# An MoE layer's experts: from split weights in three passes to unsplit fp32 weights on column tiles of 32

## The chip, the cores and the metric

The kernel runs on one NeuronCore of a Trainium2 chip. The time is that of the device, in microseconds, from launch to end: 1814.1 us, the median of three runs (1814.04, 1814.10 and 1815.13). The other seven cores do nothing. The engines are named as in the profile: PE is TensorE (matmul), PEld its loading of stationary operands, DVE is VectorE, ACT is ScalarE, POOL is GpSimd, SP is SyncE, which issues most DMAs.

## The reference

One layer: a mixer (gated linear attention and dilated attention), a router that picks 4 of 32 experts for each of 512 tokens, the experts, and a norm, all in fp32. The change touches only the experts:

```
h = xb @ w_gate_up[e] + b_gate_up[e]          # 1024 -> 2048
gate = min(h[:, ::2], 7);  up = clip(h[:, 1::2], -7, 7)
act = (up + 1) * (gate * sigmoid(1.702 * gate))
y = act @ w_down[e] + b_down[e]               # 1024 -> 1024
```

Each token's four results are weighted by its gates and added to its residual row. An expert has 12 MB of weights, 32 experts have 384 MB, and each is used by the 64 tokens that chose it on average (at most 96 in the first pass; more would go through a second path that this input does not take).

## The kernel before

The program has a mixer stage (to about 612 us), a routing part, and from 672 us the expert stage.

**Exact fp32 out of a faster type.** The mixer and the experts hold operands as float32r, which is rounded, so each fp32 operand is split in two: `hi` (the rounded value) and `lo` (the rest). A product is three passes: x_hi by w_hi, x_lo by w_hi, x_hi by w_lo. For weights the splitting costs one ACT copy (`hi`, line 1731) and one DVE subtraction (`lo`, line 1736) for every chunk of 128 x 2048 elements (1 MB).

**Chunks.** The weights of an expert come in 12 chunks: 8 of gate-up (128 input rows by 2048 outputs) and 4 of down (2 x 128 input rows by 1024 outputs). SP loads them in order into a ring of 8 buffers, `expert_chunk` (`RING`), and ACT and DVE split each into one of 4 pairs of buffers (`SLOTS`). SP may load chunk c once `lo` of chunk c-8 is done.

**Products.** `gate_up_chunk` (lines 1888, 1891) does 12 matmuls: three passes over four banks of 512 columns, with the transposed rows of the expert (`rowsT_hi`, `rowsT_lo`, 128 x 128) stationary. `down_chunk` (lines 1901, 1906) does 12 too. `turn_rows` (1852) and `turn_act` (1860) transpose the gathered rows and the activations on PE, 8 blocks of 96 each; ACT and DVE take the results out of PSUM as hi and lo. `gate_up_bias` (1881) starts the four banks with the bias.

**Bodies.** The order of work of each engine is written out by hand in `body_pe`, `body_act`, `body_dve` and the `body` functions of SP and POOL. Body e computes gate-up of expert e+1 (q = 0 to 7) and down of expert e (q = 8 to 11), and the gating of e in between. Body 0 and body 1 are written out, bodies 2 to 29 are seven turns of a loop of four bodies (`over_bodies`), body 30 is written out, and the down product of expert 31 is the last.

**Lists and rows.** The routing writes each choice (token, weight) by an indirect DMA into a table in DRAM; 16 such DMAs (`list_place`, line 1766) run on POOL at the start of the expert stage, and then the lists of all experts are read back (line 2114). From then on `list_take` on DVE gives an expert's row numbers, `gather` on POOL (1782) fetches its rows, and `scatter` (1845) adds its 96 result rows of 1024 to the residual in DRAM, one indirect DMA for each expert.

**Around it.** `mix_and_route` holds the end of the mixer, the router and the first loads of weights; `no_work` products fill PE where it would wait.

## Time and profile before

| | |
|---|---|
| median of three runs | 1814.1 us |
| profiled execution | span 1814.6 us from first to last instruction (its own time is not given apart) |
| PE busy, PEld busy | 98%, 81% of the span |
| DVE, ACT, POOL busy | 76%, 61%, 8% |
| granted PE clock | 0.993 of full speed over the span |
| moved by DMA | 497.5 MB, 274 GB/s over the span, 379 GB/s from 900 to 1700 us |
| L1736 DVE, the `lo` of the chunks | 384 of 2286 ns, 864.8 us |
| L1731 ACT, the `hi` of the chunks | 384 of 1916 ns, 735.2 us |

A busy PE is a chain of matmuls whose durations overlap: one of 512 columns is shown with some 390 ns, while the next starts 227 ns after it. So the pace of PE is read from the start times of the timeline and not from the mean of one. The name `128*128 128x512` says: a stationary operand of 128 rows by 128 columns, a moving operand of 128 by 512.

### The profile page before, as it was taken

To read this page: it belongs to the slowest core of one execution; us is meant where nothing else is said; L and a number is where in the kernel's file an instruction comes from. 1 tells how busy PE (TensorE), PEld (TensorE's weight loads), DVE (VectorE), ACT (ScalarE), POOL (GpSimd) and SP (SyncE) were. 2 spreads that over 40 slices of the span, in tenths; PEclk is the share of its full clock that TensorE was granted. 3 is DMA by queue.
4 is the path that set the end of the run, shared out by engine and by line. 5 is a ranking of instruction groups with operands and counts; after the bars stand their busy time and mean duration, and the time that the engine had idled before them with its cause. 6 is when DMAs were issued, how large, how long until landed. Compare 5 with 4: busy or idle time off the path is not lost.

```text
span 1814.6 us, 24657 instructions
## 1 busy us (share of the span) xinstructions
PE 1781.8 (98%) x9023; PEld 1469.6 (81%) x9024; DVE 1386.3 (76%) x1169; ACT 1100.3 (61%) x994; POOL 139.8 (8%) x120
## 2 busy tenths in 40 slices
PE   9999999999999999999999999999999999999996
PEld 7877788898888877788888888888888888888885
DVE  4256255537324568999999999999999999999997
ACT  4253222247422346677777777777777777777774
POOL 1000000000000026100000000000000000000001
PEclk9999999999999999999999999999999999999998
DMA  5321354312223659999999999999999999999993
GB/s 187 125 93 47 112 142 123 110 53 85 86 99 133 226 214 318 370 370 378 386 374 370 385 378 375 379 385 369 381 384 376 375 387 375 380 384 372 383 379 123
DMA packets 101688, 497.53 MB, mean 274 GB/s; under 512 B 15819, under 2 KB 17867, under 8 KB 52033
## 3 DMA queue, kind: packets, MB, share of 16 engines
q1 hardware_dynamic: 90960, 478.01, 69.2%
q0 software_dynamic: 9616, 16.62, 3.6%
q10 hardware_dynamic: 1056, 2.16, 0.5%
q8 instruction: 36, 0.59, 0.1%
q14 instruction: 20, 0.16, 0.0%
HBM read 484.85 MB, written 25.21 MB: 281 GB/s over the span
## 4 chain that ended last, share of the span: by engine, by line
PE 59%; POOL 1%; DVE 1%; DMA 1%; issue 1%; ACT 0%; DVEq 0%; POOLq 0%
PE psum L1888 24%; PE psum L1901 13%; PE psum L1891 12%; PE psum L1906 6%; POOL slots_of_experts L1766 1%; PE psum L1860 1%; PE psum L1852 1%; PE psum L1881 1%; DVE expert_lo L1736 0%; DMA slots_of_experts<-choice_token_and_weight,choice_row_of_table 0%; DMA lists_of_experts<-slots_of_experts 0%; DVE expert_chunk L2042 0%; DVE h_sb L2210 0%; POOL total_rstd L2129 0%; PE psum L2031 0%
## 5 line engine op out<-in xcount | busy, mean ns | idle before, releaser
L1736 DVE TENSOR_TENSOR expert_lo<-expert_chunk,expert_hi 128x2048 fp32r<-128x2048 f32 x384 | 864.8, 2286 | 45.7 <-ACT expert_hi L1731 43.8
L1731 ACT CAST expert_hi<-expert_chunk 128x2048 fp32r<-128x2048 f32 x384 | 735.2, 1916 | 227.3 <-PE psum L1891 170.6
L277 DVE TENSOR_TENSOR chunk_lo<-chunk,chunk_hi 128x2048 fp32r<-128x2048 f32 x48 | 110.0, 2292 | 259.0 <-ACT chunk_hi L273 240.2
L1888 PE MATMUL psum<-expert_hi,rowsT_hi 128*128 128x512 f32 x992 | 268.6, 393 | 0.0
L1891 PE MATMUL psum<-expert_lo,rowsT_hi 128*128 128x512 f32 x992 | 265.8, 390 | 0.6 <-DVE expert_lo L1736 0.6
L1888 PE MATMUL psum<-expert_hi,rowsT_lo 128*128 128x512 f32 x992 | 265.6, 390 | 0.0
L1891 PEld LDWEIGHTS psum<-expert_lo,rowsT_hi 128*128 128x128 f32 x992 | 186.1, 188 | 40.0 <-DVE expert_lo L1736 1.7
L1888 PEld LDWEIGHTS psum<-expert_hi,rowsT_lo 128*128 128x128 f32 x992 | 186.4, 188 | 39.2
L1888 PEld LDWEIGHTS psum<-expert_hi,rowsT_hi 128*128 128x128 f32 x992 | 184.0, 188 | 36.6 <-issue 0.2
L273 ACT CAST chunk_hi<-chunk 128x2048 fp32r<-128x2048 f32 x48 | 91.8, 1913 | 189.8 <-PE psum L308 158.0
L1901 PE MATMUL psum<-expert_hi,activationsT_hi 128*128 128x512 f32 x496 | 157.6, 399 | 0.0
L308 PE MATMUL psum<-xT_hi,chunk_hi 128*128 128x512 f32 x384 | 151.2, 394 | 4.6 <-DVE chunk_lo L277 2.1
L1901 PE MATMUL psum<-expert_hi,activationsT_lo 128*128 128x512 f32 x496 | 154.0, 392 | 0.0
L308 PE MATMUL psum<-xT_lo,chunk_hi 128*128 128x512 f32 x384 | 150.4, 392 | 0.0
L308 PE MATMUL psum<-xT_hi,chunk_lo 128*128 128x512 f32 x384 | 150.1, 391 | 0.0
L1906 PE MATMUL psum<-expert_lo,activationsT_hi 128*128 128x512 f32 x496 | 132.9, 390 | 0.1
L308 PE MATMUL psum<-chunk_hi,xT_hi 128*128 128x512 f32 x288 | 113.7, 395 | 2.6 <-ACT gla_v L710 1.5
L308 PE MATMUL psum<-chunk_hi,xT_lo 128*128 128x512 f32 x288 | 112.8, 392 | 0.0
L308 PE MATMUL psum<-chunk_lo,xT_hi 128*128 128x512 f32 x288 | 112.7, 391 | 0.0
L1901 PEld LDWEIGHTS psum<-expert_hi,activationsT_hi 128*128 128x128 f32 x496 | 91.2, 189 | 24.8 <-issue 6.9
L1901 PEld LDWEIGHTS psum<-expert_hi,activationsT_lo 128*128 128x128 f32 x496 | 93.8, 189 | 20.0
L1906 PEld LDWEIGHTS psum<-expert_lo,activationsT_hi 128*128 128x128 f32 x496 | 93.1, 188 | 19.9 <-DVE expert_lo L1736 0.5
(295 smaller groups left out, 1938.6 us busy)
## 6 DMA issues: line engine op xcount, KB each, us to landing
expert_chunk<-in_expert_w_gate_up SPq DMA_DIRECT2D x256, 1024.0 KB, 7.7
expert_chunk<-in_expert_w_down SPq DMA_DIRECT2D x128, 1024.0 KB, 6.9
chunk<-in_w_in SPq DMA_DIRECT2D x38, 1024.0 KB, 5.0
chunk<-in_w_branch_gla SPq DMA_DIRECT2D x4, 1024.0 KB, 5.0
chunk<-in_w_mix_out SPq DMA_DIRECT2D x4, 1024.0 KB, 5.0
gla_v<-in_x SPq DMA_DIRECT2D x4, 512.0 KB, 9.8
y_glaT_away<-h_sb SPq DMA_DIRECT2D x1, 2048.0 KB, 10.9
att_qT_then_y_glaT<-y_glaT_away SPq DMA_DIRECT2D x1, 2048.0 KB, 8.3
```

Source lines behind the costliest of these rows:

```text
L273: act.copy(self.whi[c][:], self.raw[c][:]).then_inc(self.hi_done[c], 1)
L277: dve.tensor_tensor(self.wlo[c][:], self.raw[c][:], self.whi[c][:].bitcast(F32), ALU.subtract).then_inc(self.lo_done[c], 1)
L308: last = pe.matmul(bank, stationary, moving, start=(k == 0 and n == 0), stop=(k == KT - 1 and n == 2))
L1731: act.copy(self.expert_hi[c % self.SLOTS][:], self.expert_ring[c % self.RING][:]).then_inc(self.moe["hi"], 1)
L1736: dve.tensor_tensor(self.expert_lo[s][:], self.expert_ring[c % self.RING][:], self.expert_hi[s][:].bitcast(F32), ALU.subtract).then_inc(se ...
L1766: pool.indirect_dma_start(self.table, bass.IndirectOffsetOnAxis(ap=self.address[:, b, j:j + 1], axis=0), self.record[:, b, j, :], None, bo ...
L1852: last = pe.transpose(turned(f)[:, k, :], rows[taken, (HALF_KT * f + k) * P:(HALF_KT * f + k + 1) * P], self.ident[taken, taken])
L1860: last = pe.transpose(turned(f)[:, k, :], a[taken, (HALF_KT * f + k) * P:(HALF_KT * f + k + 1) * P], self.ident[taken, taken])
L1888: pe.matmul(bank, x[:, k, :], whi[s][:, m // 2, m % 2 * COLS:(m % 2 + 1) * COLS], start=False, stop=False)
L1891: last = pe.matmul(bank, rows_hi[:, k, :], wlo[s][:, m // 2, m % 2 * COLS:(m % 2 + 1) * COLS], start=False, stop=(k == KT - 1))
L1901: pe.matmul(bank, x[:, 2 * q + kk, :], whi[s][:, kk, m * COLS:(m + 1) * COLS], start=(q == 0 and kk == 0 and x is acts[0]), stop=False)
L1906: last = pe.matmul(bank, acts[0][:, 2 * q + kk, :], wlo[s][:, kk, m * COLS:(m + 1) * COLS], start=False, stop=(q == 3 and kk == 1))
```

## The change

The weights of the experts are no longer split. PE multiplies them as fp32, and the stationary operand is a group of 32 token rows instead of 128: `FIRST_SLOTS` is 96, so there are three groups (`GROUPS`), and for each group four products stand side by side on four column tiles of the array (`PARTS`), each with its own block of the weights as moving operand and its own 32 partitions of one PSUM bank as output. Gate-up moves 512 columns for each, down 256.

- `hi`, `lo`, their buffers and the hi/lo copies of rows and activations are gone; ACT alone takes transposed rows and activations out of PSUM. The ring has 16 buffers instead of 8, and SP waits for PE's use of chunk c-16 (`used`) instead of `lo` of c-8.
- The outputs now lie by part of the columns: partition 32p+r, group j holds token 32j+r and part p. So the gating works on 128 x 768 instead of 128 x 1024 elements, `turn_act` is six blocks of 128 (four behind q = 2, two behind q = 3), and the result rows leave in pieces of 256 columns: three indirect DMAs for each expert, which add to a residual seen as 2048 rows of 256. The row numbers of the pieces come from four more reads of the lists and one DVE operation.
- The last expert's down product stays row by row (96 stationary columns, 512 moving, fp32), for its result is added through one-hot products.
- In `mix_and_route`, SP loads three chunks when the first half of the last mixing product is done, three more behind the last bank, and two at the start of the expert stage, and no chunk is split there.

```diff
-                for c in range(1, self.SLOTS):
-                    self.hi(act, c)
...
-    RING, SLOTS = 8, 4
+    RING = 16
...
+    PARTS, GROUPS = P // QUARTER, FIRST_SLOTS // QUARTER
+    PIECE = D_MODEL // PARTS
...
+    def chunk_here(self, pe, c, i=0):
+        pe.wait_ge(self.chunk_loaded[c % self.RING], 16 * (self.PER_TURN // self.RING) * i + 16 * (c // self.RING + 1))
+        return self.expert_ring[c % self.RING]
...
+        def scatter(pool, e, u):
+            pool.wait_ge(S["y_out"], G * e + G)
+            pool.wait_ge(S["pieces"], 2 * e + 2)
+            pool.wait_ge(S["scattered"], 16 * G * e)
+            for j in range(G):
+                pool.sem_inc(S["passed"], 1)
+                pool.indirect_dma_start(pieces, bass.IndirectOffsetOnAxis(ap=self.piece_row[u][:, j:j + 1], axis=0),
+                                        y[:, j * PIECE:(j + 1) * PIECE], None, bounds_check=self.last_piece, oob_is_err=False,
+                                        compute_op=ALU.add).then_inc(S["scattered"], 16)
...
+        def gate_up_chunk(pe, c, i, k, x=xT):
+            w = chunk_here(pe, c, i)
+            for j, bank in enumerate(h_banks):
+                for p in range(PARTS):
+                    last = pe.matmul(bank[part_rows(p), :], x[:, k, part_rows(j)], w[:, p // 2, p % 2 * COLS:(p % 2 + 1) * COLS],
+                                     start=False, stop=(k == KT - 1))
+            last.then_inc(S["used"], 1)
+
+        def down_chunk(pe, c, i, q):
+            w = chunk_here(pe, c, i)
             for kk in range(2):
...
+                for j in range(G):
+                    for p in range(PARTS):
+                        last = pe.matmul(y_of(j)[part_rows(p), :], aT[:, q, kk, part_rows(j)], w[:, kk, p * PIECE:(p + 1) * PIECE],
+                                         start=(q == 0 and kk == 0), stop=(q == 3 and kk == 1))
+            last.then_inc(S["used"], 1)
...
+        def last_down_chunk(pe, c, q):
+            w = chunk_here(pe, c)
             for kk in range(2):
...
+                for m, bank in enumerate(last_banks):
+                    last = pe.matmul(bank[taken, :], as_act(xT)[:, q, kk, :], w[:, kk, m * COLS:(m + 1) * COLS],
+                                     start=(q == 0 and kk == 0), stop=(q == 3 and kk == 1))
+            last.then_inc(S["used"], 1)
...
-                        sp.wait_ge(S["lo"], TURN * i + c - RING + 1)
+                        sp.wait_ge(S["used"], TURN * i + c - RING + 1)
...
+                for p in range(PARTS):
+                    pool.dma_start(self.piece_lists[part_rows(p)].rearrange("p j e n -> p j (e n)"),
+                                   self.table[E:(FIRST_SLOTS + 1) * E, :].rearrange("(j p e) n -> p j (e n)", j=G, e=E)
+                                   ).then_inc(S["lists_in"], 16)
```

On PE, in body 1 (gate-up of expert 2), stood before, from the second chunk to the fifth:

```order
L1888 MATMUL psum<-expert_hi1,rowsT_hi 128x512 x4
L1888 MATMUL psum<-expert_hi1,rowsT_lo 128x512 x4
L1891 MATMUL psum<-expert_lo1,rowsT_hi 128x512 x4
L1888 MATMUL psum<-expert_hi2,rowsT_hi 128x512 x4
L1888 MATMUL psum<-expert_hi2,rowsT_lo 128x512 x4
L1891 MATMUL psum<-expert_lo2,rowsT_hi 128x512 x4
L1860 MATMUL psum<-identity_sb,h_sb 128x96 x8
L1888 MATMUL psum<-expert_hi3,rowsT_hi 128x512 x4
L1888 MATMUL psum<-expert_hi3,rowsT_lo 128x512 x4
L1891 MATMUL psum<-expert_lo3,rowsT_hi 128x512 x4
```

and now, from the second chunk to the fifth (an output of 32 partitions, 12 products for each chunk; line 1888 is now `turn_act`):

```order
L1915 MATMUL psum<-expert_chunk5,rowsT 32x512 x12
L1915 MATMUL psum<-expert_chunk6,rowsT 32x512 x12
L1888 MATMUL psum<-identity_sb,h_sb 128x128 x4
L1915 MATMUL psum<-expert_chunk7,rowsT 32x512 x12
L1888 MATMUL psum<-identity_sb,h_sb 128x128 x2
L1915 MATMUL psum<-expert_chunk_late0,rowsT 32x512 x12
```

The 12 products of a chunk are as many as before; the transposes are split over two places. On PE, around the rows of the next expert and its bias in the same body (the down chunks), there stood before:

```order
L1906 MATMUL psum<-expert_lo1,activationsT_hi 128x512 x4
L1852 MATMUL psum<-identity_sb,h_sb 128x96 x8
L1881 MATMUL psum<-bias_rows1,ones_r 128x512 x4
L1901 MATMUL psum<-expert_hi2,activationsT_hi 128x512 x2
L1901 MATMUL psum<-expert_hi2,activationsT_lo 128x512 x2
```

and now:

```order
L1924 MATMUL psum<-expert_chunk_late3,activationsT 32x256 x24
L1924 MATMUL psum<-expert_chunk_late7,activationsT 32x256 x24
L1878 MATMUL psum<-identity_sb,h_sb 128x96 x8
L1908 MATMUL psum<-bias_rows1,bias_place_r 128x512 x3
L1924 MATMUL psum<-expert_chunk_late4,activationsT 32x256 x24
L1924 MATMUL psum<-expert_chunk_late5,activationsT 32x256 x24
```

A down chunk is 24 products of 256 columns, and the bias three products. On POOL, from the lists to the first scatter, there stood before:

```order
L2103 MEMSET activationsT_hi 128x8x32
L2103 MEMSET activationsT_lo 128x8x32
L2103 MEMSET rowsT_hi 128x8x32
L2103 MEMSET rowsT_lo 128x8x32
L1766 DMA slots_of_experts<-choice_token_and_weight,choice_row_of_table 4128x2 x4
L1782 DMA h_sb<-normed_rows,row_index 128x1024
L1766 DMA slots_of_experts<-choice_token_and_weight,choice_row_of_table 4128x2 x12
L2114 DMA lists_of_experts<-slots_of_experts 128x64
L1782 DMA h_sb<-normed_rows,row_index 128x1024 x2
L1845 DMA residual_rows<-h_sb,row_index 512x1024
```

and now:

```order
L1776 DMA slots_of_experts<-choice_token_and_weight,choice_row_of_table 4128x2 x4
L1796 DMA h_sb<-normed_rows,row_index 128x1024
L1776 DMA slots_of_experts<-choice_token_and_weight,choice_row_of_table 4128x2 x12
L2131 DMA lists_of_experts<-slots_of_experts 128x64
L2134 DMA lists_by_quadrant<-slots_of_experts 32x3x64 x4
L1796 DMA h_sb<-normed_rows,row_index 128x1024
L1870 DMA residual_rows<-h_sb,piece_row 2048x256 x3
```

The clearing of unused slots is gone, the lists are read five times, and the scatter of body 0 stands in body 0 and no longer in body 1.

## Rows read from the trace of the kernel before

**Rows 1.** the page: busy time and share of the span of each engine
```profile
PE 1781.8 (98%) x9023; PEld 1469.6 (81%) x9024; DVE 1386.3 (76%) x1169; ACT 1100.3 (61%) x994; POOL 139.8 (8%) x120
```

**Rows 2.** windows: stretch, length, busy us (instructions) per engine, PEclk, DMA share, GB/s
```profile
625.00:640.00 15.00, 15.00 (x71) 12.61 (x70) 10.01 (x17) 8.36 (x17) 2.09 (x2) 1.00 1.01 423
1200.00:1300.00 100.00, 100.00 (x476) 82.35 (x475) 95.58 (x65) 75.82 (x54) 7.88 (x6) 1.00 0.99 379
```

**Rows 3.** timeline, PE, one body: start us, us, engine, line, operation
```profile
1202.67 0.82 PE L1860 MATMUL psum<-identity_sb,h_sb 96*128 96x96 f32 x8
1206.11 1.07 PE L1888 MATMUL psum<-expert_hi,rowsT_hi 128*128 128x512 f32 x4
1208.83 1.07 PE L1888 MATMUL psum<-expert_hi,rowsT_hi 128*128 128x512 f32 x4
1222.43 0.82 PE L1852 MATMUL psum<-identity_sb,h_sb 96*128 96x96 f32 x8
1223.19 0.50 PE L1881 MATMUL psum<-bias_rows,ones_r 32*128 32x512 f32 x4
1237.36 0.82 PE L1860 MATMUL psum<-identity_sb,h_sb 96*128 96x96 f32 x8
```

**Rows 4.** timeline, PE, line 556: fp32 products on tiles of 64 columns
```profile
169.81 0.38 PE L556 MATMUL psum<-w_lr,gla_qkT 128*64 128x256 f32 x1
169.81 0.38 PE L556 MATMUL psum<-scan_keep_sb,gla_qkT 128*64 128x256 f32 x1
170.02 0.38 PE L556 MATMUL psum<-w_lr,gla_qkT 128*64 128x256 f32 x1
```

**Rows 5.** timeline, PE, lines 1048, 1015 and 1020: tiles of 64 and 32 columns
```profile
382.49 0.40 PE L308 MATMUL psum<-chunk_hi,xT_lo 128*128 128x512 f32 x1
382.82 0.71 PE L1015 MATMUL psum<-att_kT_window,att_qT_window 64*32 64x256 f32 x20
383.45 0.71 PE L1020 MATMUL psum<-att_kT,att_qT_then_y_glaT 64*128 64x128 f32 x8
...
400.99 1.09 PE L1048 MATMUL psum<-qk_halves_then_probsT,att_v 128*64 128x128 f32 x24
403.30 0.33 PE L1032 MATMUL psum<-identity_sb,att_negated 128*128 128x128 f32 x1
```

**Rows 6.** timeline, PE: router products and transposes on the whole array
```profile
642.08 1.87 PE L1414 MATMUL psum<-router_w_sb,chunk 128*128 128x32 f32 x16
643.78 1.19 PE L1403 MATMUL psum<-identity_sb,h_sb 128*128 128x128 f32 x8
644.72 0.47 PE L308 MATMUL psum<-chunk_hi,xT_hi 128*128 128x512 f32 x1
```

**Rows 7.** waits of SyncE, 860 to 1780: us in total, times, longest us
```profile
SPq L1726 <- DVE expert_lo L1736: 692.4, 314, 4.1
```

**Rows 8.** DMA queues, 900 to 1700: packets, MB, share of 16 engines
```profile
q1 hardware_dynamic: 40211, 290.51, 92.5%
q0 software_dynamic: 6727, 12.35, 6.0%
q14 instruction: 1, 0.01, 0.0%
```

**Rows 9.** timeline, PE, at the start of the expert stage
```profile
672.84 0.51 PE L1881 MATMUL psum<-bias_rows,ones_r 32*128 32x512 f32 x4 [0.93 <-PEq L139]
703.25 1.20 PE L1888 MATMUL psum<-expert_hi,rowsT_hi 128*128 128x512 f32 x4
```

**Rows 10.** timeline, POOL: two of the 16 DMAs of line 1766
```profile
682.23 0.98 POOL L1766 DMA_INDIRECT slots_of_experts<-choice_token_and_weight,choice_row_of_table  x1 [0.30 <-issue]
709.41 3.03 POOL L1766 DMA_INDIRECT slots_of_experts<-choice_token_and_weight,choice_row_of_table  x1 [0.30 <-issue]
```

**Rows 11.** timeline, PE and POOL: the last expert's down product and the last scatter
```profile
1783.69 0.62 PE L1901 MATMUL psum<-expert_hi,rowsT_hi 128*128 128x512 f32 x2
1785.96 2.18 POOL L1845 DMA_INDIRECT residual_rows<-h_sb,row_index  x1 [9.70 <-ACT h_sb L1950]
```

More of the change, by code:

```diff
@@ L93, in shape_constants @@
     c["bias_row"] = e
+    c["quadrant"] = (np.arange(P) // QUARTER).astype(np.float32)[:, None].copy()
+    place = np.zeros((P, P), np.float32)
+    for g in range(FIRST_SLOTS // QUARTER):
+        for part in range(P // QUARTER):
+            place[g * QUARTER + 2 * part:g * QUARTER + 2 * part + 2, part * QUARTER:(part + 1) * QUARTER] = 1.0
+    c["bias_place"] = place
     return c
@@ L1326, in _ @@
                 for b in range(NB):
+                    if b == NB - 1:
+                        sp.wait_ge(R["halfway"], 1)
+                        for q in range(3):
+                            self.load_gate_up(sp, self.body_chunk(0, q), 1, q)
                     sp.wait_ge(self.bank_free[b], last_mix + 1)
@@ L1330, in _ @@
                     sp.dma_start(self.normed[b * P:(b + 1) * P, :], hn[b]).then_inc(self.normed_stored, 16)
+                sp.wait_ge(self.bank_full[NB - 1], last_mix + 1)
+                for q in range(3, 6):
+                    self.load_gate_up(sp, self.body_chunk(0, q), 1, q)
             @block.gpsimd
@@ L1719, in load_bias_rows @@
         rows = self.bias_rows[u % 2]
-        for s in range(2):
-            sp.dma_start(rows[s:P:P // 4, :], self.bias_table[bass.ds(e, 1), :, s, :].rearrange("a m n -> (a m) n")
+        for j in range(self.GROUPS):
+            sp.dma_start(rows[j * QUARTER:j * QUARTER + 2 * self.PARTS, :],
+                         self.bias_table[bass.ds(e, 1), :, :, :].rearrange("a m s n -> (a m s) n")
                          ).then_inc(self.bias_in[u % 2], 16)
@@ L1854, in turn_rows, with turn_act @@
                 last.then_inc(S["x_turned"], 1)
-        def turn_act(pe, e):
+        def turn_act(pe, e, groups):
             pe.wait_ge(S["act"], e + 1)
-            for f in range(2):
-                for k in range(HALF_KT):
-                    last = pe.transpose(turned(f)[:, k, :], a[taken, (HALF_KT * f + k) * P:(HALF_KT * f + k + 1) * P],
-                                        self.ident[taken, taken])
-                last.then_inc(S["act_turned"], 1)
-        def turned_hi(act, e, in_bank, done, dst):
-            for f in range(2):
-                act.wait_ge(in_bank, 2 * e + f + 1)
-                act.copy(dst[:, HALF_KT * f:HALF_KT * (f + 1), taken], turned(f)).then_inc(done, 1)
@@ L1895, in down_chunk @@
-        def down_chunk(pe, c, i, q, banks=y_banks, acts=self.actT):
-            s = c % SLOTS
-            pe.wait_ge(S["hi"], TURN * i + c + 1)
-            for kk in range(2):
-                for x in acts:
-                    for m, bank in enumerate(banks):
-                        pe.matmul(bank, x[:, 2 * q + kk, :], whi[s][:, kk, m * COLS:(m + 1) * COLS],
-                                  start=(q == 0 and kk == 0 and x is acts[0]), stop=False)
-            pe.wait_ge(S["lo"], TURN * i + c + 1)
+            for j in groups:
+                if j >= 2:
+                    pe.wait_ge(S["aT_out"], G * e + j - 1)
+                for k in range(2):
+                    last = pe.transpose(turned_act(j)[:, k * P:(k + 1) * P], a[:, (2 * j + k) * P:(2 * j + k + 1) * P],
+                                        self.ident[:])
+                last.then_inc(S["act_turned"], 1)
@@ new lines, in down_chunk @@
+        def down_chunk(pe, c, i, q):
+            w = chunk_here(pe, c, i)
+            for kk in range(2):
+                for j in range(G):
+                    for p in range(PARTS):
[4 more added lines that the diff above has]
+            w = chunk_here(pe, c)
@@ L1904, in down_chunk @@
             for kk in range(2):
-                for m, bank in enumerate(banks):
-                    last = pe.matmul(bank, acts[0][:, 2 * q + kk, :], wlo[s][:, kk, m * COLS:(m + 1) * COLS], start=False,
-                                     stop=(q == 3 and kk == 1))
-            last.then_inc(S["slots_free"], 1)
+                for m, bank in enumerate(last_banks):
+                    last = pe.matmul(bank[taken, :], as_act(xT)[:, q, kk, :], w[:, kk, m * COLS:(m + 1) * COLS],
+                                     start=(q == 0 and kk == 0), stop=(q == 3 and kk == 1))
@@ L2030, in hi_products @@
                 pe.wait_ge(S["y_hi"], m + 1)
-                pe.matmul(sums[b][:, m, :], hotT[:, b, :], y_hi[:, m * COLS:(m + 1) * COLS], start=False, stop=False)
+                pe.matmul(sums[b][:, m, :], hotT[taken, b, :], y_hi[taken, m * COLS:(m + 1) * COLS], start=False, stop=False)
         def lo_products(pe, b):
@@ L2035, in lo_products @@
                 pe.wait_ge(S["y_lo"], m + 1)
-                last = pe.matmul(sums[b][:, m, :], hotT[:, b, :], y_lo[:, m * COLS:(m + 1) * COLS], start=False, stop=True)
+                last = pe.matmul(sums[b][:, m, :], hotT[taken, b, :], y_lo[taken, m * COLS:(m + 1) * COLS], start=False, stop=True)
             last.then_inc(S["totals"], 1)
```

333 lines of the change are left out of this document (150 added, 183 removed).

## The prediction

> **What bounds the kernel now.** I read the page first: PE is busy for 98% of the span [rows 1]. Then the windows, because the experts take 1,110 us of the span and a mean over all stages hides them. In 100 us of the expert loop PE is busy for 100.00, DVE for 95.58 and ACT for 75.82, and the granted clock is 1.00, the 2.4 GHz level [rows 2]. The DMA share of 0.99 looks like a second bound, so I read the waits: SP stood 692.4 us, 314 times, waiting for a free buffer [rows 7]. A loader that waits is not the bound; its transfers wait for their turn in the queues' time. In the mixer the same queues moved 423 GB/s, against 379 here [rows 2]. So PE sets the pace, DVE is close behind, and the DMA has some 10% in hand.
>
> The pace comes from start times, since the records of matmuls overlap. One body, from one transposing of activations to the next, is 1237.36 − 1202.67 = 34.69 us. A chunk of weights is 1208.83 − 1206.11 = 2.72 us. Twelve chunks are 32.64, and 2.05 are left for transposes and bias (1223.19 − 1222.43 = 0.76 for the rows alone) [rows 3].
>
> **What an fp32 product costs.** Two places in the mixer show it. On two tiles of 64 columns, two products of 256 columns start together at 169.81 and the next at 170.02 [rows 4]: about 0.213 us for one pass over 256 columns. Line 1015 issues 10 products in the code and shows 20 records [rows 5], so an fp32 product is two passes. These ten hold 2,048 columns (six of 256, four of 128); in two passes one after another they would take 4,096/256 × 0.213 = 3.4 us, but the next line starts 0.63 us after them (383.45 − 382.82). So tiles with different weights and different moving data do run side by side, 5.4 at once here.
>
> **The change part by part.**
>
> *Gate-up chunk.* Three groups × two passes × 512 columns, four tiles at once: 6 × 0.43 = 2.58 us. *Down chunk:* two halves × three groups × two passes × 0.215 = 2.58. Both were 2.72. The array does less work than 12 passes of split products by about 5%, if four tiles always stand side by side.
>
> *Rest of a body.* Six transposes of 128: eight of them took 644.72 − 643.78 = 0.94 us [rows 6], so six take 0.71. The rows' transposes stay at 0.76. The bias is three products that take a step of 0.43 if their twelve records pair up as in a chunk. New are three returns between the whole array and tiles of 32. At 382.49 a whole-array product was followed by tiles after 0.33 us [rows 5], against 0.227 for a product of its size (2.72/12), so 0.1 at least; I take 0.25 each for a drain and a first weight load that nothing covers, 0.75 in all. Body: 12 × 2.58 + 0.71 + 0.76 + 0.43 + 0.75 = 33.6 us. With 0.1 or 0.45 for a return it is 33.2 or 34.2.
>
> *DVE and ACT.* Per chunk a DVE subtraction of 2.3 us and an ACT copy of 1.9 go (384 of each). Neither sets the pace before, so it earns nothing by itself, but DVE has room for whatever the new gating needs. The gating handles 128 x 768 elements instead of 128 x 1024, in a body where DVE and ACT now idle for most of the time.
>
> *SP and the ring.* SP waits for PE's chunk c−16 instead of `lo` of c−8: 16 chunks of lead are over 40 us at 2.58 a chunk. The loads per body are 12 MB; at 423 GB/s they take 12 × 1.049/0.423 = 29.7 us, and at the packets' own share (92.5% of 800 us for 290.51 MB [rows 8]) 32.0. Gathers and scatters add 6.0% of 34.69 = 2.1 [rows 8]. So the queues need 31.8 to 34.1 us for a body and PE 33.6. That is the closest second, and the ring covers its jitter.
>
> *Start.* The bias products stand at 672.84 and wait for their sequencer, and body 0 begins at 703.25 [rows 9]. Expert 0's eight chunks end 8 × 0.14 = 1.1 us sooner, and the transposes and first chunk need no splitting by ACT and DVE ahead (about 1 us for the first): I take −2.5, with −1 and −4 as ends. The lists: one of POOL's 16 placing DMAs took 0.98 us, another 3.03 where DVE was subtracting [rows 10]. With most subtractions gone the list is out some 8 us sooner. Reading it five times instead of once adds four issues of about 1 us; the rows of the next expert are needed only in the middle of body 0, so this hides. If the 8 us don't come, about 3 us of body 0 stand open.
>
> *Bodies.* The last down product starts at 1783.69 [rows 11]: 1783.69 − 703.25 = 1,080.4 us for 31 bodies, or 31 × 34.69 + 5.0 of waits. Afterwards 31 × 33.6 = 1,041.6: −38.8 against the whole, if the 5 us of waits go with their cause; at 33.2 it is −51, at 34.2 −20.
>
> *Tail.* The last down product is now 16 products of 512 columns in fp32: 16 × 2 × 0.43 = 13.8 us against 4 × 2.72 = 10.9, +2.9, and +0.3 for changes of tile. The scatter before the last (one issue, 2.18 us, after 1783.69 [rows 11]) becomes three of 256 columns. Two more issues put its end some 4 to 5 us later in a tail of 1814.6 − 1783.69 = 30.9 us, in which PE's 13.8 come first; I count it hidden, with 1.5 us in hand, and +3 as its price if not.
>
> *Code.* Each half of a product is a weight load and a matmul of its own, and smaller tiles need four times as many: 12 chunks × 24 or 48 passes make some 384 pairs in a body against 144 + transposes. Before, the queue of instructions moved one packet in 800 us [rows 8], so code fetched at the loop's turns cost PE nothing visible. With twice the code a turn can need a fetch that PE waits for. The nearest row for such a wait is 0.93 us on PE's sequencer [rows 9]; I take 1.2 for each of six turns, +7, with 0 and 20 as ends. The Trainium skill (Runtime: NRT & Kernel Launch, Instruction fetch mechanics) says that PE's instruction memory holds 2,048 instructions and that a taken branch to a target outside the window must fetch before it goes on. By that rule the four bodies of a turn did not fit before either, yet no row here shows a stall, so it changes only the weight of a rival below.
>
> *Sum.* 1814.6 − 2.5 − 38.8 + 2.9 + 0.3 + 7 = 1783.5 in the profiled execution's terms (span 1814.6). The median of the runs is 0.5 lower: 1783 to 1784, say 1784. Bounds of the costs above give 1770 to 1795.
>
> **The rivals.**
>
> *A. Refetch at each turn.* Every turn of the loop waits for its first code and once or twice again: 3.3 us × 6 = 20 instead of 7. That gives 1797. For: the code grows. Against: one instruction packet in 800 us [rows 8].
>
> *B. Issue of pairs decides: slower.* A down chunk needs 48 pairs of weight load and matmul in 2.58 us, one per 54 ns; gate-up needs one per 107. The point from which it decides is 54 ns, and the gain is eaten at about 60: 192 down pairs × 6.4 ns = 1.2 us of each body. Against it: between 400.99 and 403.30 PE passed the 24 records of line 1048 and, as after 382.82, the 20 and 8 of lines 1015 and 1020: 52 pairs in 2.31 us, or 44 ns each [rows 5]. For it: the eight records of line 1020 fill about 0.65 us (81 ns each), what is left of the 2.31 when 24 and 20 take some 1.66 of it, and 16 router products of just 32 columns took 642.08 to 643.78, 1.70 us, 106 ns each, far more than their columns [rows 6]. At 81 ns a body is 192 × 0.027 = 5.2 us longer: +161, near 1945. Were it 62 ns, a body would grow by 192 × 0.008 = 1.6 and the whole come to 1833. The Trainium skill (TensorE: Matmul & The Clock Gate, Wait — 56ns, not 53.3ns?) gives about 62 ns per matmul for a sequencer without hardware decode and a floor near 25 with it; the 44 ns above speak for the second.
>
> *C. Tiles not side by side all the time.* If the weight load of a tile can't hide under that tile's own product (32 columns, some 55 ns), each of the 8 × 6 + 4 × 12 = 96 steps of a body pays: 5.3 us a body, near 1945. If only two tiles ran at once, a body would double, to over 2,700. Rows 5 speak against both.
>
> *D. The DMA becomes the bound.* 34.1 us at the upper end is 0.5 above PE: +16, about 1800. It is dear only if a scattered piece of 1 KB costs the queues as much as a row of 4 KB, for there are now four times as many: then scatters alone grow from about 1.3 to 5 us, a body is 38, and the time near 1860.
>
> *E. A wait once a body.* A chain of gather, scatter or gating that was covered comes late by about 1 us in each: 1784 + 31 = 1815, in the band 1805 to 1830. For: three scatters on POOL, each with a wait. Against: POOL is busy for 8% [rows 1], and DVE and ACT have more room than before.
>
> **How the numbers follow.** Forecast 0.56 (1770 to 1795), A 0.12, B 0.09, C 0.06, D 0.08, E 0.09. The likeliest gives 1784. The range: 1764 below, a body of 33.2 and no cost of code, less a few us for the start; 1836 above, which takes in A, E, the mild half of D and B at 62 ns, and leaves about 0.18 out above. A measurement of this kernel can tell 0.2%, that is 3.6 us. Faster: 0.56 + 0.12, a third of D and less than half of E, with some of B's lower end, 0.77 to 0.78. Same: 0.04, the part of E near 1814. Slower: the rest, 0.18.
>
> **What would show it.** Starts of the activation transposes 33.6 us apart; chunks 2.58 apart; in a chunk four products starting together, every 0.43 us in gate-up and 0.215 in down (not together: C; a down chunk longer than a gate-up chunk: B). SP's waits now on PE and long; if they vanish and PE waits for chunks, D. Instruction packets inside the loop with gaps in PE at the turns, 1 us each, or 3 in A. PE waiting for ACT, DVE or POOL once a body is E. The tail from the last down product's start 33 to 34 us instead of 30.9. Wrong altogether would be a body above 34.69.

## The result, and the profile after

The changed kernel takes 1831.2 us (median of four runs, 1829.6 to 1832.8) against 1814.6 for the kernel before (1814.0 to 1816.3). The ratio is 1.0092, with a 95% interval of 1.0078 to 1.0106: slower by 0.9%, where 1784 was forecast. The profiled executions have spans of 1831.0 and 1814.6 us, so 16.4 us are to be explained, and 47 between the forecast (1783.5 in these terms) and the result.

The page of the kernel after, first the busy line, then the queues:

```profile
span 1831.0 us, 38017 instructions
...
PE 1767.4 (97%) x16447; PEld 996.1 (54%) x16448; DVE 449.8 (25%) x692; ACT 378.9 (21%) x673; POOL 218.1 (12%) x182
...
q1 hardware_dynamic: 92272, 479.12, 68.4%
q0 software_dynamic: 18672, 16.74, 4.5%
...
q8 instruction: 140, 2.29, 0.5%
```

DVE and ACT are nearly free, as expected; PE is not [rows 1]. The last line is code: 140 packets of 16 KB, for which the prediction had budgeted 7 us. Between 900 and 1700 us the kernel before moved one instruction packet [rows 8]; this one moved 87:

```profile
q1 hardware_dynamic: 39985, 284.29, 90.2%
q0 software_dynamic: 12680, 11.73, 7.2%
q8 instruction: 86, 1.41, 0.7%
q14 instruction: 1, 0.01, 0.0%
```

An average body says little here, so I listed the distance between the first transposes of successive bodies. Before, it is 34.7 from body 1 on. After, it is 33.6, except at six places, one behind each turn of the loop but the last: 41.5, 40.5, 42.2, 39.7, 41.5 and 41.0 us. The timeline of PE, first an ordinary body (the products of the next would start at 1198.2 by the same pattern), then what stands at a turn of the loop:

```profile
1172.35 0.66 PE L1888 MATMUL psum<-identity_sb,h_sb 128*128 128x128 f32 x4
1172.94 2.78 PE L1915 MATMUL psum<-expert_chunk,rowsT 128*32 128x512 f32 x24
1175.65 0.44 PE L1888 MATMUL psum<-identity_sb,h_sb 128*128 128x128 f32 x2
1176.02 10.51 PE L1915 MATMUL psum<-expert_chunk_late,rowsT 128*32 128x512 f32 x96
1186.35 5.36 PE L1924 MATMUL psum<-expert_chunk_late,activationsT 128*32 128x256 f32 x96
1191.64 0.88 PE L1878 MATMUL psum<-identity_sb,h_sb 96*128 96x96 f32 x8
1192.45 0.50 PE L1908 MATMUL psum<-bias_rows,bias_place_r 32*128 32x512 f32 x3
1192.88 5.39 PE L1924 MATMUL psum<-expert_chunk_late,activationsT 128*32 128x256 f32 x96
1204.60 1.93 PE L1915 MATMUL psum<-expert_chunk,rowsT 128*32 128x512 f32 x8 [6.33 <-issue]
```

(The last row is cut by the window; the start time and the wait are what is read.) Four gate-up chunks take 1186.35 − 1176.02 = 10.33, 2.58 each, and two down chunks 5.29, 2.65 each. Then PE stands still for 6.33 us, and what ended the wait is "issue": no semaphore, no engine, no DMA of data.

What PE was doing is on record one level lower. Every engine closes a turn with a branch instruction (COMPARE_BRANCH, on the line of the loop). The trace gives, for the six jumps back, the shortest, median and longest duration in ns. First the kernel before, then the kernel after, PE and for comparison ACT:

```profile
L2051 PEldq COMPARE_BRANCH  x6: 211/211/224, 913.0 to 1606.9; - x6
```

```profile
L2065 PEldq COMPARE_BRANCH  x6: 5557/6034/7367, 913.4 to 1622.4; - x6
L2065 ACTq COMPARE_BRANCH  x6: 45/45/50, 915.1 to 1624.1; - x6
```

Of the engines only PE is held at the jump (DVE, POOL and SP take under 0.1 us for theirs too). Its branch takes 0.21 us before and 5.6 to 7.4 after, 6.16 on the mean. When the branch begins, 20 matmul records are still ahead of it and last another 1.36 us; the rest is the wait that the timeline shows, 4.5 to 6.3 us. In each of these branches one packet of code begins 3.2 to 5.0 us after the branch (917.21 for the one at 913.42), takes about 1 us, and the branch ends some 1.4 to 1.5 us after it (919.55).

At the turn near 915 the wait is 5.06 us. The windows there (columns as in rows 2):

```profile
914.00:920.00 6.00, 0.94 (x20) 0.37 (x16) 0.00 (x0) 1.20 (x3) 2.63 (x2) 0.88 1.00 388
920.00:925.00 5.00, 5.00 (x28) 1.21 (x28) 0.00 (x0) 0.00 (x0) 3.12 (x3) 0.50 0.50 83
925.00:930.00 5.00, 5.00 (x52) 1.38 (x44) 0.00 (x0) 0.00 (x0) 0.00 (x0) 0.97 0.75 253
```

PE had been idle for 5 us, and the granted clock then is 0.50, the 1.2 GHz level, for the five microseconds in which PE works again: 28 matmul records (two for each fp32 product) instead of some 46. So a turn costs the wait and then another 1.7 to 2.9 us, 2.4 on the mean.

The other loss is ahead of the loop. Timeline of PE in the gate-up of expert 0:

```profile
687.27 7.56 PE L1915 MATMUL psum<-expert_chunk,activationsT 128*32 128x512 f32 x63
695.22 1.08 PE L1915 MATMUL psum<-expert_chunk,activationsT 128*32 128x512 f32 x5 [0.38 <-issue]
696.66 1.06 PE L1915 MATMUL psum<-expert_chunk,activationsT 128*32 128x512 f32 x4 [0.37 <-issue]
698.08 0.49 PE L1878 MATMUL psum<-identity_sb,h_sb 96*128 96x96 f32 x4 [0.35 <-issue]
700.20 0.64 PE L1878 MATMUL psum<-identity_sb,h_sb 96*128 96x96 f32 x3 [1.63 <-issue]
701.63 0.32 PE L1878 MATMUL psum<-identity_sb,h_sb 96*128 96x96 f32 x1 [0.80 <-issue]
702.35 8.27 PE L1915 MATMUL psum<-expert_chunk,activationsT 128*32 128x512 f32 x48 [0.40 <-issue]
...
713.13 1.06 PE L1915 MATMUL psum<-expert_chunk_late,rowsT 128*32 128x512 f32 x8
```

From 694.8 to 702.3 PE's products come in handfuls with waits on nothing visible between them. SP stops as well: the chunk of SP's next load was free from 692.6 on, and the load was issued at 700.93. In these 7 us the queues move next to nothing, so it is no lack of bandwidth (the last columns are the granted clock, 0.86, the DMA share, 0.21, and 46 GB/s):

```profile
695.00:702.00 7.00, 3.59 (x17) 1.40 (x16) 0.00 (x0) 0.00 (x0) 5.28 (x6) 0.86 0.21 46
```

Behind the stall the granted clock is 0.51 from 700 to 707 us, and the 48 records that start at 702.35 take 8.2 us instead of 5.3. Earlier, PE waits 3.52 us ahead of its bias products at 672.88, where it had waited 0.93 before [rows 9], and then has a granted clock of 0.50 from 673 to 679 us, where it was 1.00 before.

Where the 16.4 us are, against rows 9 and 11 and the end of the span:

| stretch | before | after | difference | forecast |
|---|---|---|---|---|
| first product of body 0 | 703.25 | 713.13 | +9.9 | −2.5 |
| from there to the last down product | 1080.4 | 1085.8 | +5.3 | −31.8 |
| from there to the end | 30.9 | 32.1 | +1.2 | +3.2 |

The middle line is 31 × 33.6 = 1041.6 us of bodies, 38.8 less than before, and 44.8 us at six turns of the loop.

### The profile page after: what moved, and what is told of

Read it like the earlier page. It is cut to its first block, busy times and chain, and to the rows that moved or that the text cites. A ratio compares the mean times of both kernels' runs of the same rounds, so it can differ in the third digit from the quotient of the medians.

```text
span 1831.0 us, 38017 instructions
## 1 busy us (share of the span) xinstructions
PE 1767.4 (97%) x16447; PEld 996.1 (54%) x16448; DVE 449.8 (25%) x692; ACT 378.9 (21%) x673; POOL 218.1 (12%) x182
## 4 chain that ended last, share of the span: by engine, by line
PE 61%; issue 2%; DVE 0%; POOL 0%; ACT 0%; DVEq 0%
PE psum L1915 38%; PE psum L1924 18%; PE psum L1888 2%; PE psum L1878 1%; PE psum L1908 1%; PE psum L1932 1%; PE psum L244 0%; DVE expert_chunk L2056 0%; DVE h_sb L2212 0%; POOL total_rstd L2147 0%; PE psum L2045 0%; PE psum L2039 0%; ACT up_values L2168 0%; DVE gate_values L2212 0%; PE psum L2237 0%
## 5 line engine op out<-in xcount | busy, mean ns | idle before, releaser
L1915 PE MATMUL psum<-expert_chunk,rowsT 128*32 128x512 f32 x2976 | 341.9, 611 | 30.7 <-issue 30.7
L1915 PE MATMUL psum<-expert_chunk_late,rowsT 128*32 128x512 f32 x2976 | 328.5, 593 | 0.0
L1870 POOL DMA_INDIRECT residual_rows<-h_sb,piece_row x93 | 145.4, 1564 | 903.9 <-ACT h_sb L1981 830.0
L1915 PEld LDWEIGHTS psum<-expert_chunk,rowsT 128*32 128x32 f32 x2976 | 97.1, 112 | 243.9 <-issue 242.2
L1915 PEld LDWEIGHTS psum<-expert_chunk_late,rowsT 128*32 128x32 f32 x2976 | 93.4, 110 | 202.9 <-issue 200.5
L1924 PE MATMUL psum<-expert_chunk_late,activationsT 128*32 128x256 f32 x3072 | 172.2, 380 | 0.0
L1924 PE MATMUL psum<-expert_chunk,activationsT 128*32 128x256 f32 x2880 | 161.3, 380 | 0.0
L1924 PEld LDWEIGHTS psum<-expert_chunk_late,activationsT 128*32 128x32 f32 x3072 | 98.1, 110 | 73.8 <-issue 13.6
L1924 PEld LDWEIGHTS psum<-expert_chunk,activationsT 128*32 128x32 f32 x2880 | 92.1, 110 | 69.3 <-issue 12.6
L321 PEld LDWEIGHTS psum<-xT_hi,chunk_hi 128*128 128x128 f32 x384 | 72.1, 188 | 21.3 <-DVE chunk_lo L290 2.7
```

Of the source, the lines that this page charges most:

```text
L321: last = pe.matmul(bank, stationary, moving, start=(k == 0 and n == 0), stop=(k == KT - 1 and n == 2))
L1870: pool.indirect_dma_start(pieces, bass.IndirectOffsetOnAxis(ap=self.piece_row[u][:, j:j + 1], axis=0), y[:, j * PIECE:(j + 1) * PIECE], No ...
L1915: last = pe.matmul(bank[part_rows(p), :], x[:, k, part_rows(j)], w[:, p // 2, p % 2 * COLS:(p % 2 + 1) * COLS], start=False, stop=(k == KT ...
L1924: last = pe.matmul(y_of(j)[part_rows(p), :], aT[:, q, kk, part_rows(j)], w[:, kk, p * PIECE:(p + 1) * PIECE], start=(q == 0 and kk == 0), ...
```

## The experiments

Theory F: the long distances are PE waiting for its own code. From one branch to the next, PE has 3,241 instructions in the trace after (1,604 matmuls, 1,604 weight loads, 33 others) against 1,383 before, which were not fetched again at a turn. (The counts in the expectations below differ from the traces by up to three.) Theory P for the start: the twelve placing DMAs of POOL, which now go out without a pause, delay the fetching of code for PE and SP.

The runs with a ratio are medians of four executions. The others were executed once, and what is read from them is in the distances and waits of their traces. `...` in a diff marks lines left out.

**The loop written out.**

```diff
-            with engine.Fori(0, TURNS) as i:
-                for u in range(self.UNROLL):
-                    body(engine, PEELED + u, i)
-            for e0 in range(PEELED + self.UNROLL * TURNS, LAST):
+            for e0 in range(PEELED, LAST):
                 body(engine, e0, 0)
```

> The changed kernel with bodies 2 to 29 written out instead of seven turns of four; every instruction of a body is the same. Theory F (a turn of the loop, 3,240 PE instructions against 1,385 before, no longer stays in PE's instruction memory, and the jump back waits for code): all distances between the first transposes of successive bodies are 33.6 us, the six of 39.7 to 42.2 are gone (44.8 us), body 0 still starts at about 713, time about 1786. Rival R (code cannot be fetched fast enough beside a DMA share of 0.98, jump or no jump): waits of PE stay, spread over the bodies, time near 1831.

Measured: 1788.6 us, ratio to before 0.9853 (0.9833 to 0.9872). Every distance is 33.6 us, and the turn near 915 is gone. PE's timeline of this kernel, and its instruction packets from 900 to 1700:

```profile
909.68 5.39 PE L1924 MATMUL psum<-expert_chunk_late,activationsT 128*32 128x256 f32 x96
914.89 7.91 PE L1915 MATMUL psum<-expert_chunk,rowsT 128*32 128x512 f32 x72
```

```profile
q8 instruction: 75, 1.23, 0.6%
q14 instruction: 9, 0.07, 0.0%
```

There are nearly as many packets as in the loop (84 against 87), so it is not fetching that costs, but fetching after a jump back. Written in a line, code comes in time, even at 393 GB/s and a DMA share of 1.02. Rival R falls. The start is unchanged (body 0 at 713.43).

**Turns of two bodies.** With a ring of 12, since 24 chunks are no multiple of 16; the lines left out fit the first loads and the row numbers of the pieces to it.

```diff
-    RING = 16
-    GU, PER_BODY, UNROLL = 8, 12, 4
+    RING = 12
+    GU, PER_BODY, UNROLL = 8, 12, 2
...
```

> The changed kernel with 14 turns of two bodies (1,620 PE instructions a turn) and, so that buffers come out even, a ring of 12 chunks; the row numbers of the pieces are taken one body ahead instead of two. Theory F with a memory that holds a turn of 1,620: no instruction packets of PE inside the loop, no long distances, time about 1786 like the unrolled one. If a turn of 1,620 does not fit either: 13 jumps of 6 to 8 us, time 1875 to 1890. Rival G (the six long distances come from something else that happens every fourth body, such as the order in which ring buffers come round): they stay at every fourth body, 1831. A ring of 12 alone should cost nothing, since SP waits 2.4 us for nearly every chunk.

Measured: 1881.2 us, ratio 1.0378 (1.0360 to 1.0396). All 13 jumps cost: 39.6 to 42.2 us at every second body, 33.6 between, 97 packets from 900 to 1700. The loss follows the jump, not the position of a body among four (rival G falls), and a turn of 1,623 instructions (1,620 in the expectation) did not stay in the memory.

**The kernel before with turns of 14 bodies.**

```diff
-    GU, PER_BODY, UNROLL = 8, 12, 4
+    GU, PER_BODY, UNROLL = 8, 12, 14
...
-            dve.wait_ge(self.moe["scattered"], 16 * (e - self.UNROLL + 1))
+            dve.wait_ge(self.moe["scattered"], 16 * (e - 3))
```

> The kernel before, its products untouched, with bodies 2 to 29 as two turns of 14 bodies (some 4,850 PE instructions a turn) instead of seven turns of four. Theory F: instruction packets appear all through the loop, and at its one jump back PE waits 5 to 6 us and then runs at the lower clock for a while, so one distance between bodies is some 41 to 43 us instead of 34.7; time about 1822. Rival H (the stall belongs to the tiled fp32 products and the ring of 16): no long distance, time 1814.

Measured: 1818.0 us. Packets appear in the loop (33 on q8, and 30 smaller ones on q14, for code of other engines), and one distance, at the one jump, is 37.7 instead of 34.7. So the split kernel pays too, but 3.0 us and not 6 to 8. Its timeline, its branch and a window there:

```profile
1260.18 1.07 PE L1906 MATMUL psum<-expert_lo,activationsT_hi 128*128 128x512 f32 x4
1263.91 1.19 PE L1888 MATMUL psum<-expert_hi,rowsT_hi 128*128 128x512 f32 x4 [2.67 <-ACT expert_hi L1731]
```

```profile
L2051 PEldq COMPARE_BRANCH  x1: 6454/6454/6454, 1257.2 to 1257.2; - x1
```

```profile
1262.00:1267.00 5.00, 3.09 (x13) 2.55 (x14) 5.00 (x4) 2.78 (x4) 0.00 (x0) 1.00 0.91 350
```

The wait is 2.67 us, and the granted clock stays 1.00. It is put down to ACT, which had a longer wait than usual at its own jump (3.58 us). But PE needed only the cast of this chunk, the 201st, and that had ended at 1256.48. PE was held by its own branch, for 6.45 us, no less than in the changed kernel. What differs is the work ahead of the branch: 17 matmul records last 4.08 us here, for a wide product takes 0.227 us, and 20 last 1.36 us there, where four narrow ones run at once. The same hold is covered for two thirds in the one kernel and for a fifth in the other, and only the longer wait was followed by a lower clock.

**A quarter of the weights' bytes in the queues.**

```diff
+        if 16 <= c < 368:
+            sp.dma_start(self.expert_ring[r][0:QUARTER], src[0:QUARTER]).then_inc(self.chunk_loaded[r], 16)
+            return
```

> The changed kernel with its loop of four bodies, but chunks 16 to 367 load only 32 of their 128 partitions (the products use old values in the rest), so the queues are a quarter as busy with weights. If the code that PE fetches after the jump waits behind weight packets: each long distance between bodies shrinks from 39.7 to 42.2 to about 36 to 37 us, body 33.6 elsewhere, time about 1800 to 1806. If the wait is the fetch itself, whatever else the queues carry: long distances stay at 40 to 42, time 1825 to 1831. In both the short distances stay 33.6 if PE and not the DMA sets the pace of a body; if the DMA does, they fall.

Measured: 1815.4 us, between the two forecasts. Long distances are 37.7 to 38.6, others 33.6 at 109 GB/s. The jump near 915 and the clock behind it:

```profile
917.30 9.81 PE L1918 MATMUL psum<-expert_chunk,rowsT 128*32 128x512 f32 x72 [2.95 <-issue]
```

```profile
917.00:922.00 5.00, 4.70 (x28) 1.61 (x32) 0.00 (x0) 0.00 (x0) 4.33 (x3) 0.66 0.46 56
```

```profile
L2068 PEldq COMPARE_BRANCH  x6: 3652/3908/4017, 913.1 to 1608.3; - x6
```

The wait near 915 falls from 5.06 to 2.95 us; three chunks behind it still take 9.74 us instead of 7.84. With all the weights a jump costs 7.5 us on the mean, 5.1 of wait and 2.4 at the lower clock; here it is 4.6, of which 2.8 and 1.8. The branch takes 3.87 us on the mean instead of 6.16, and the packets show where the 2.3 us are: the packet of code begins 1.2 us after the branch instead of 3.8, and once begun takes no less time (1.1 us instead of 1.0). So some 2.5 us are code waiting its turn beside the weights; the rest of the hold is there at a DMA share of 0.43 too. That a body stays at 33.6 with a quarter of the traffic shows that PE sets its pace and the DMA does not.

**How long a turn may be.** Thirty instructions that do nothing, in each body of the kernel before:

```diff
+                if q == 4:
+                    for _ in range(30):
+                        pe.nop()
```

> The kernel before with 30 instructions that do nothing added to PE's code in each body, so that a turn of four bodies has some 1,505 PE instructions instead of 1,385 (a turn of 1,620 did not stay in the memory, one of 1,385 did). The added instructions themselves cost at most 1 us a body. If the limit lies below 1,505: instruction packets inside the loop and every fourth distance about 3 us longer (as at the one jump of the 14-body turn), time 1832 plus the instructions. If it lies above: no instruction packets, all distances equal.

Measured: 1813.1 us, no packets. But the turn takes 138.77 us as before and the trace has no such instruction, so this run tested nothing. With semaphore increments in their place, 28 and 45 a body:

```diff
+                if q == 4:
+                    for _ in range(28):
+                        pe.sem_inc(self.padding, 1)
```

> The kernel before with 28 semaphore increments added to PE's code in each body (the instructions that did nothing in the run before left no trace, so they tested nothing), which makes a turn of four bodies some 1,497 PE instructions. They cost at most 0.5 us a body. If a turn of 1,497 stays in the memory: no instruction packets inside the loop, distances equal, about 35.2 at most. If not: packets all through the loop and every fourth distance 3 us longer, as at the one jump of the 14-body turn.

> The same with 45 increments a body, a turn of some 1,565 PE instructions. It brackets the limit from above: with theory F and the changed kernel's 1,620 that did not stay, I expect packets in the loop and every fourth distance 3 us longer, time about 1814 + 18 + 31 times what the increments cost. If both this and 1,497 stay, the limit lies between 1,565 and 1,620, or the limit is not a count of instructions.

Measured: 1828.1 and 1949.5 us, one packet on q8 in each between 900 and 1700, and no long distance at every fourth body: turns of 1,495 and 1,563 instructions still stay, and PE's branch takes 0.21 us in both. My forecast for 45 was wrong on that. The time itself is another thing, which I had not foreseen. Increments follow each other at 0.151 us, so 28 take 4.2 us and 45 take 6.8, and PE's sequencer works ahead of the array. The first are covered but for 0.45 us a body, the second leave PE idle for 2.75 us in every body, and a little later the clock falls (1.91 us for four products where 1.07 is usual):

```profile
1111.92 1.19 PE L1889 MATMUL psum<-expert_hi,rowsT_hi 128*128 128x512 f32 x4 [2.75 <-ACT expert_hi L1732]
1112.94 1.56 PE L1889 MATMUL psum<-expert_hi,rowsT_lo 128*128 128x512 f32 x4
1114.30 1.91 PE L1892 MATMUL psum<-expert_lo,rowsT_hi 128*128 128x512 f32 x4
```

**The two-body turn, 64 instructions shorter.** Two groups of down products are left out of each body; the lines left out are those of the two-body run above.

```diff
...
                 for j in range(G):
+                    if kk == 1 and q in (1, 2) and j == 2:
+                        continue
```

> The kernel with 14 turns of two bodies and a ring of 12, without two groups of four down products in each body (their part of the result is left out), so that a turn has 1,556 PE instructions instead of 1,620. A kernel before with a turn of 1,564 fetched nothing in its loop. Theory F with a limit between 1,564 and 1,620: no instruction packets in the loop, no long distance, each body 33.6 less 2 x 0.43 = 32.7 us, time about 1875 - 13 x 7.5 - 31 x 0.87, near 1753, in any case below 1765. If it is not the number of instructions that decides (the tiled products, or the jump itself in this kernel): the 13 long distances of 39 to 41 us stay, time near 1848.

Measured: 1757.5 us, 124 us less than the median with those products. All distances are 32.7 up to the last three (32.8, 33.5, 33.2), the clock is 1.00, from 900 to 1700 there is one packet on q8, and the branch is as short as in the kernel before:

```profile
q1 hardware_dynamic: 43101, 306.65, 94.4%
q0 software_dynamic: 13939, 12.92, 7.4%
q8 instruction: 1, 0.02, 0.0%
```

```profile
L2067 PEldq COMPARE_BRANCH  x13: 207/208/236, 837.4 to 1622.3; - x13
```

Same jumps, same products, same ring: apart from the 16 products left out, 64 instructions of 1,623, nothing differs. This settles theory F; the limit lies between 1,563 and 1,623. The 31 bodies account for 31 × 0.87 = 27 of the 124 us, the 13 jumps for 95. (At 32.7 us a body the queues move 399 GB/s, and in the last bodies PE waits three times for a chunk, up to 0.27 us: the DMA is that near.)

**The placing DMAs spaced.**

```diff
                     for j in range(TOP_K):
+                        pool.wait_ge(S["used"], (b - 1) * TOP_K + j + 1)
                         self.list_place(pool, b, j, last)
```

> The changed kernel, in which the twelve placing DMAs of POOL behind the early gather each wait for one more chunk of PE, so that they come one in 2.6 us instead of one in 1.3. Theory P (the stalls of PE and SP between 694.8 and 702.3 come from back-to-back indirect DMAs on POOL that delay the fetching of code): body 0 starts at about 705 instead of 713, with later lists, so PE may wait for the gathered rows late in body 0 for 5 to 10 us; time 1825 to 1835. Rival Q (a fetch that is late for a reason that has nothing to do with POOL): PE still trickles near 695 to 702 and body 0 starts at 713; time 1835 to 1845.

Measured: 1829.8 us. No handfuls, and body 0 starts at 704.94 instead of 713.13. The price comes where it was expected: the lists are later, and the first distance is 41.0 us. PE's code is the same, so the stall comes with the pace of POOL's DMAs, and rival Q falls. That it is the fetching of code which they hold up, the other half of theory P, is not shown, and two things speak against it. At the jumps PE stands still until a packet has come, while here it goes on in handfuls. And in the kernel with the loop written out the one packet of PE's code between 690 and 704 us has landed at 696.3, in the changed kernel at 698.6, and the handfuls go on until 704.5 and 702.3.

**Loop written out, and groups of three.**

```diff
...
+                        pool.wait_ge(S["used"], 2 * (((b - 1) * TOP_K + j) // 3) + 1)
                         self.list_place(pool, b, j, last)
```

> Bodies written out, and the twelve placing DMAs in groups of three, each group held until PE has used two more chunks (1.7 us for one on the mean, instead of 1.3 without a pause and 2.6 in the spaced run). Theory P (an unbroken run of some six indirect DMAs delays the fetching of code, and a pause ends that): no trickle of PE near 695, body 0 starts at about 705 to 706, and the lists come early enough that the first distance between bodies is 33.6 or at most 2 us more; time 1779 to 1782. If the mean pace alone decides, and 1.7 us is still too fast: the trickle stays in part and body 0 starts later than 708; time 1783 to 1790.

Measured: 1780.2 us, ratio to before 0.9806 (0.9790 to 0.9823), the fastest of the kernels that compute everything. Every distance is 33.6, the first too. POOL and PE in the stretch where the handfuls ("trickle" in the expectations) were:

```profile
695.36 0.98 POOL L1776 DMA_INDIRECT slots_of_experts<-choice_token_and_weight,choice_row_of_table  x1 [0.30 <-issue]
698.32 0.98 POOL L1776 DMA_INDIRECT slots_of_experts<-choice_token_and_weight,choice_row_of_table  x1 [1.98 <-remote]
```

```profile
689.52 9.00 PE L1915 MATMUL psum<-expert_chunk,activationsT 128*32 128x512 f32 x72
698.45 0.88 PE L1878 MATMUL psum<-identity_sb,h_sb 96*128 96x96 f32 x8
699.26 5.36 PE L1915 MATMUL psum<-expert_chunk,activationsT 128*32 128x512 f32 x48
```

The first two groups went out without a pause between them (688.88 to 696.34), and three chunks took 8.93 us there instead of 7.86 in the spaced run: a trace of the same stall. Body 0 starts at 707.14, a microsecond later than forecast.

**Loop written out, even pauses.**

```diff
...
+                        for n in range(2):
+                            pool.memset(self.spare[:], 0.0).then_inc(S["paused"], 1)
+                            pool.wait_ge(S["paused"], 2 * (TOP_K * (b - 1) + j) + n + 1)
                         self.list_place(pool, b, j, last)
```

> Bodies written out, and two short clears of an unused tile ahead of each of the twelve placing DMAs, so that POOL issues one in about 2.1 us, evenly, without waiting for PE. Theory P: no trickle, body 0 at about 705; the lists come at some 720, the gathered rows for expert 2 may be 1 to 3 us late; time 1780 to 1784. If what matters is that POOL has no idle moment (it works through the pauses here), the trickle stays: body 0 at 712, time 1787.

Measured: 1787.6 us, ratio 0.9851. One DMA in 2.4 us, no handfuls, body 0 at 704.68: it is the indirect DMAs close together that hurt, not a POOL that is always busy. But the rows of expert 2 are 8 us late and not 1 to 3, and the first distance is 44.2:

```profile
740.24 1.54 PE L1878 MATMUL psum<-identity_sb,h_sb 96*128 96x96 f32 x8 [8.34 <-DMA h_sb<-normed_rows,row_index]
```

## Why the prediction was wrong, point by point

- **What bounds the kernel: right.** PE set the pace before and after; the light run shows that the DMA does not, and emptying DVE and ACT brought no time by itself.
- **The cost of an fp32 product and of a body: right.** 33.6 us forecast, 33.6 measured in every body but six. Two passes, four tiles side by side and a weight load that hides under its neighbours were read correctly from rows 4 and 5. A chunk of down products takes 2.65 instead of 2.58, the changes of shape cost less than my 0.75 (2.35 us of a body are left for all that is not a chunk, where I had 2.65), so two small errors cancel. B, C, D and E did not come about; the 55 ns that C puts on a weight load stand in no run.
- **Code: the step that failed, by its size.** I put 1.2 us on each of six turns, 7 in all, with 20 as upper end; it was 7.5 each, 44.8 in all, and this alone turns a gain into a loss. I took the price of a wait from rows 9, which have no jump in them. Rival A named the mechanism, but its 3.3 us a turn had no row behind it either; that the split kernel pays about as much at a jump (3.0) is luck. Two things were missing. The hold is some 6 us in both kernels, and I did not ask how much queued work would cover it: 1.4 us of narrow products against 4.1 of wide ones. Nor did I ask what the clock does after the wait: it falls, and the first chunks are 1.7 to 2.9 us slower.
- **Code, the argument about the memory: wrong.** I wrote that four bodies did not fit before either. The count was never made: a turn had 1,383 instructions, and rows 2 would have given it, 476 + 475 in 100 us or some 1,320 in the 138.8 us of a turn. The Trainium skill (Runtime: NRT & Kernel Launch, Instruction fetch mechanics) gives 2,048 for PE and says that a taken branch outside the window forces a fetch. The traces agree with the rule in kind (1,383 stays, 3,241 does not), not with the number as a limit for a loop: 1,563 stays and 1,623 does not. By my own 384 pairs in a body a turn has over 3,000 instructions; counted properly, a refetch at each turn would have been the forecast, though at A's price the forecast would still have been 1797.
- **Start: wrong in sign.** I counted POOL's faster placing DMAs as a gain of 8 us for the lists, which would be hidden. They did become faster: 0.98 us each instead of up to 3.03 [rows 10], one in 1.29 us instead of one in 2.1, and the lists were read at 706.8 instead of 717.2. But PE and SP were held up beside them: +9.9 instead of −2.5. That DVE's subtractions had been spacing them is an inference from rows 10. Some 8 of the 12 us between forecast and result go with this stall, for body 0 starts at 704.7 to 704.9 without it. That is still 1.5 later than before and not 2.5 earlier: expert 0's first products follow a wait of 3.5 us, at a granted clock of 0.50.
- **Tail: right in kind.** Last down product 1812.69 − 1798.88 = 13.8 us as forecast; the end is 1.2 us later than before and not 3.2.
- **The DMA** had less in hand than the 10% I wrote, as my 31.8 to 34.1 us for a body already said: at 32.7 us a body and 399 GB/s PE begins to wait for chunks now and then.

What stays open: what makes the packet of code begin 3 to 5 us late beside the weights, and by what path indirect DMAs issued on POOL hold up PE and SP while the queues are nearly empty. The runs show that spacing ends it, not how it works. Whether the limit also depends on where the loop's code begins in a packet of 16 KB was not tested, and a two-body turn under 1,563 instructions that leaves nothing out was not tried.

## What to carry to other kernels

Count the instructions that a change puts into a loop, engine by engine, and compare with the instruction packets of the trace: packets inside a loop, waits that end on "issue" behind the jump, and a branch of 6 us instead of 0.2 mean that the loop no longer stays in memory. Writing it out gave 2.3% here, and the fetching in line cost nothing that shows. Narrow tiles multiply instructions for the same work (here 1,604 matmul records a turn instead of 656), and they shorten the queued work that could cover a hold. When a slow engine is freed, look at what its slowness had been spacing.

## What the runs showed of the hardware that was not expected

- PE's code for a loop of up to 1,563 recorded instructions was not fetched again; at 1,623 it was (97 packets of 16 KB from 900 to 1700 us), and each jump cost 6 to 8.6 us.
- PE's branch at a jump back took 0.21 us without a fetch, and with one 5.4 to 7.4 us beside 350 GB/s or more of loads, whatever the shape of the products, and 3.7 to 4.0 us beside 109 GB/s.
- Fetching in a straight line cost nothing that shows, at 84 packets in 800 us beside 393 GB/s.
- A semaphore increment on PE takes 0.151 us of its sequencer; about 4 us of them were hidden behind the array's work.
- Indirect DMAs of 128 small rows, one in 1.3 us, held up PE and SP from about the seventh on, for 7.5 us; one in 2.4 us did not.
- After idle times of PE of 5 us the granted clock was 0.50 for some 5 us; after one of 2.95 it was 0.66 over the next 5 us (the run with few bytes), and after one of 2.75 too (45 increments a body); after one of 2.67 in the kernel before with 14-body turns it stayed 1.00.
